# Hybrid decoder step on one core: expert section in one block with the router, stick-breaking attention and the front of the delta rule in one block, and a last expert pair of its own

## The reference, cut to what matters

```python
h = rms_norm(x, norm_mix); proj = h @ w_in          # columns: gated delta rule q k v z beta a, stick-breaking q k v
# delta rule, 8 heads x 64, in chunks of 64 tokens:
decay = exp(G_i - G_j)                              # G: cumulated log decays
low   = strict_lower(beta * k k^T * decay)          # t_inv = (I + low)^-1
qk    = lower(q k^T * decay)
u, w  = t_inv @ (v * beta), t_inv @ (k * beta * exp(G))
# then the state recurrence over 4 chunks, per-head norm, gate silu(z)
# stick-breaking attention: z = q k^T / 8 + b, A[t,s] = sigmoid(z[t,s]) * prod_{s<j<t} sigmoid(-z[t,j]), o = A v
#   (sampled tokens: over 1024 cached keys and values read by page; prompt: within its 256 tokens)
x = x + concat(o_delta, o_attention) @ w_out
# 32 experts, top 4 per token:
hu = t @ w_up[e] + b_up[e]; act = (up + 1) * gate * sigmoid(1.702 * gate); y = act @ w_down[e] + b_down[e]
x = x + sum_e gate_weight * y;  output rms_norm(x, norm_final)
```

## Time and profile before

| what | us |
|---|---|
| median of 3 runs | 1319.24 (1318.08 to 1328.87) |
| the profiled execution, its own time | 1323.29 |
| its span, first to last instruction | 1321.7 |
| TensorE busy | 1254.5 (95%) |
| VectorE, ScalarE, GpSimd busy | 406.7, 240.7, 92.2 |
| moved by DMA | 463.58 MB, mean 351 GB/s |

### The profile page before, as it was taken

The page is one execution under the profiler, slowest core; times in us unless marked ns, Lnnn a source line. Parts: engine busy times, 40 slices in busy tenths (PEclk is TensorE's granted clock), DMA queues, the critical chain, the costliest instruction groups (busy, mean ns, idle before and its releaser), DMA issues.

```text
span 1321.7 us, 19961 instructions
## 1 busy us (share of the span) xinstructions
PE 1254.5 (95%) x7888; PEld 571.3 (43%) x7888; DVE 406.7 (31%) x921; ACT 240.7 (18%) x402; POOL 92.2 (7%) x167
## 2 busy tenths in 40 slices
PE   8999999799999999999999999999999999999996
PEld 6777766587433333333333333333333333333332
DVE  4721424552742222322122232212213222222224
ACT  3222333323211011110111011011101101010103
POOL 6101141152000000000000000000000000000000
PEclk9999998889989999999999999999999999999999
DMA  9643699100779999999999999999999999999993
GB/s 324 229 133 112 219 387 360 30 20 7 286 264 381 429 427 428 428 428 429 428 428 428 428 428 428 429 428 429 428 428 429 428 428 428 428 428 429 428 428 139
DMA packets 66105, 463.58 MB, mean 351 GB/s; under 512 B 16654, under 2 KB 16782, under 8 KB 41478
## 3 DMA queue, kind: packets, MB, share of 16 engines
q1 hardware_dynamic: 62808, 452.22, 83.4%
q0 software_dynamic: 3200, 10.49, 2.1%
q10 hardware_dynamic: 46, 0.18, 0.0%
HBM read 459.15 MB, written 3.70 MB: 350 GB/s over the span
## 4 chain that ended last, share of the span: by engine, by line
PE 47%; DMA 23%; DVE 1%; issue 1%; SPq 0%; ACT 0%; POOLq 0%; POOL 0%; DVEq 0%; ACTq 0%
PE bank L2064 28%; DMA ring<-in_w_up 20%; PE bank L2081 6%; PE bank L2033 4%; PE bank L2012 4%; DMA hoT<-in_w_down 2%; PE bank L2016 1%; PE bank L2037 1%; PE bank L2108 1%; PE bank L2053 0%; PE bank L2089 0%; PE bank L2119 0%; SPq L750 0%; DVE work L2297 0%; DVE X L2292 0%
## 5 line engine op out<-in xcount | busy, mean ns | idle before, releaser
L2064 PE MATMUL bank<-ring,work 128*64 128x512 f32 x1536 | 340.1, 597 | 14.6 <-DMA ring<-in_w_up 14.6
L2064 PEld LDWEIGHTS bank<-ring,work 128*64 128x64 f32 x1536 | 109.3, 137 | 242.8 <-issue 230.5
L2081 PE MATMUL bank<-ring,work 128*64 128x512 f32 x768 | 173.0, 596 | 7.4 <-ACT work L2171 5.5
L410 PE MATMUL bank<-hoT,ring 128*128 128x288 f32 x448 | 113.0, 407 | 1.1 <-ACT hoT L445 0.8
L2064 PE MATMUL bank<-work 128*64 128x512 f32 x256 | 112.9, 594 | 0.0
L2064 PE MATMUL bank<-hoT,work 128*64 128x512 f32 x256 | 112.9, 594 | 0.0
L2263 DVE TENSOR_SCALAR work<-bank 128x512 f32<-128x512 f32 x32 | 21.9, 683 | 257.8 <-PE bank L2064 257.8
L2081 PEld LDWEIGHTS bank<-ring,work 128*64 128x64 f32 x768 | 55.7, 137 | 103.0 <-issue 99.1
L410 PEld LDWEIGHTS bank<-hoT,ring 128*128 128x128 f32 x448 | 83.5, 190 | 23.2 <-ACT hoT L445 0.9
L2155 ACT ACTIVATE work<-bank 128x1024 f32<-128x1024 f32 x16 | 16.4, 1023 | 383.2 <-PE bank L2016 383.2
L2225 DVE TENSOR_TENSOR X<-X,bank 128x512 f32<-128x512 f32 x64 | 44.0, 688 | 108.6 <-PE bank L2033 108.6
(11 more groups left out here) (396 smaller groups left out, 1315.5 us busy)
## 6 DMA issues: line engine op xcount, KB each, us to landing
ring<-in_w_up SPq DMA_DIRECT2D x96, 2048.0 KB, 24.6
ring<-in_w_down SPq DMA_DIRECT2D x48, 2048.0 KB, 26.9
work<-in_w_up SPq DMA_DIRECT2D x16, 2048.0 KB, 25.8
hoT<-in_w_up SPq DMA_DIRECT2D x16, 2048.0 KB, 30.1
work<-in_w_down SPq DMA_DIRECT2D x8, 2048.0 KB, 25.1
hoT<-in_w_down SPq DMA_DIRECT2D x8, 2048.0 KB, 29.4
ring<-in_w_in SPq DMA_DIRECT2D x7, 2048.0 KB, 16.7
ring<-in_cache_k SPq DMA_DIRECT2D x48, 256.0 KB, 3.1
```

What stands on the lines that cost most here:

```text
L410: ins = pe.matmul(bank[0:m, i % 2, 0:T], w[:, k, :], hT[:, k, :], start=k == 0, stop=k == KD - 1)
L2064: ins = pe.matmul(bank[CAP * e:CAP * e + CAP, g, :], xT[:, k, CAP * e:CAP * e + CAP], weight(odd, ch + e, k % 2 * RSLOT + 512 * g), start= ...
L2081: ins = pe.matmul(bank[CAP * e:CAP * e + CAP, 4 + m, :], aT[:, k, CAP * e:CAP * e + CAP], weight(odd, ch + e, k % 4 * D + 512 * m), start= ...
```

## The change

Four things.

- **No barrier before the expert section.** Its streams follow the router's in the same block. In the barrier's place stand waits: all five engines wait for `s_passes` (the number of passes is written), GpSimd clears its two buffers once the second tile's choice is made, SyncE loads the last norm's weight once the six norm rows are made, VectorE waits for the stored states only before it writes the first activation. The two spare products at the end of the router (`keep_busy(2, 2)`) are gone.
- **Attention and delta-rule front joined.** What stood at the head of block 4 now stands among the attention's work of block 3: `decay_columns`, `decay_rows(i)`, `products(c)` on TensorE, each through bank 7 of PSUM; `copy_rows`, `exp_differences` on ScalarE; `differences`, `take_products`, `lower` on VectorE; three additions and the first level's masks on GpSimd. Keys and values are both turned into bank 6 and both copied by ScalarE (`copy_kv`); `scale_v` is gone, and GpSimd scales the values later, in block 4. Eight spare products stand at three places of the joined block. Some of its tiles lie in the ring, in the buffer of chunk 3, so chunk 3 is now loaded at the head of block 4. There ScalarE makes the row exponentials from a copy in one activation of 1280 columns (`eR`), after the copies of `turn_T`. The biases of the experts are loaded after the heads' norm, before chunks 0, 1 and 6.
- **One more unit of the cache by GpSimd** (unit 11).
- **The last pair by itself.** TensorE's loop runs one turn less, and the last two pairs stand behind it. In the very last, the gather and turn for a pair that does not come are left out, and prompt tile 0 of X is put into banks 6 and 7, where its last outputs are accumulated; ScalarE squares and VectorE scales it from there. For all pairs, the last two slices of `up` are done by halves of the columns. The final norm's operations are in another order, with fused ones for the sampled tokens and tile 0.

```diff
-        BY_POOL = [m for m in range(12, 32) if m % 2]
+        BY_POOL = [m for m in range(11, 32) if m % 2]
...
-                sp.wait_ge(s_ringfree, U_WO)
-                load_chunk(sp, 0, 3)
...
+                def decay_columns():
+                    for i, (mp, md) in enumerate(((U2, dU2), (Us2, dUs2))):
+                        pe.matmul(bank[:, 7, NU * i:NU * i + 16], mp, gg[:, 0:16], start=True, stop=True)
+                        ins = pe.matmul(bank[:, 7, NU * i + 16:NU * (i + 1)], md, gg[:, 16:NU], start=True, stop=True)
+                    ins.then_inc(d_R, 1)
+
+                def decay_rows(i):
+                    g = GROUPS[i]
+                    if i:
+                        pe.wait_ge(d_D, i)
+                        pe.wait_ge(d_eGT, i)
+                    else:
+                        pe.wait_ge(d_Gs, 1)
+                    pe.wait_ge(d_pool, i + 1)
+                    pe.matmul(bank[:, 7, 0:width(g)], blk64, Lm[:, cols(g)], start=True, stop=True).then_inc(d_R, 1)
+
+                def products(c):
+                    if c:
+                        pe.wait_ge(d_QK, c)
+                    else:
+                        pe.wait_ge(d_D, 3)
+                        pe.wait_ge(d_eGT, 3)
+                    for p in range(HP):
+                        for a in range(2):
+                            ins = pe.matmul(bank[pr(a), 7, P * p:P * p + P], gq[pr(a), 4 + p, tk(c)], gq[pr(a), p:p + 5:4, tk(c)],
+                                            start=True, stop=True)
+                    ins.then_inc(d_KK, 1)
...
                 scores(0)
+                decay_columns()
                 scores(1)
+                decay_rows(0)
                 turn_kv(0)
                 turn(0)
                 turn_kv(1)
                 values(0)
+                decay_rows(1)
                 turn(1)
                 scores(2)
+                decay_rows(2)
+                values(1)
                 turn_kv(2)
-                values(1)
+                products(0)
                 turn(2)
                 scores(3)
+                products(1)
+                values(2)
                 turn_kv(3)
-                values(2)
+                products(2)
+                keep_busy(3)
                 turn(3)
                 turn_kv(4)
                 values(3)
+                products(3)
+                keep_busy(1)
+                products(4)
+                keep_busy(4)
...
                 betas(0)
                 betas(1)
-                copy_k(0)
+                copy_kv(0)
+                copy_rows(0)
                 copy_A(0)
-                copy_k(1)
+                copy_kv(1)
+                copy_rows(1)
                 copy_A(1)
                 betas(2)
-                copy_k(2)
+                copy_rows(2)
+                exp_differences(0)
+                exp_differences(1)
+                copy_kv(2)
                 copy_A(2)
                 betas(3)
-                copy_k(3)
+                copy_kv(3)
                 copy_A(3)
-                copy_k(4)
+                copy_kv(4)
+                exp_differences(2)
...
+                def differences(i):
+                    g = GROUPS[i]
+                    u0, u1 = GRP[g]
+                    dve.wait_ge(d_R, i + 2)
+                    dve.tensor_tensor(un(QK)[:, u0:u1], un(bank[:, 7, 0:width(g)]), ubc(Gs, u0, u1), ALU.subtract).then_inc(d_D, 1)
+                    dve.wait_ge(d_D, i + 1)
+                    dve.scalar_tensor_tensor(out=un(E1)[:, u0:u1], in0=un(QK)[:, u0:u1], scalar=-1.0,
+                                             in1=mbc((nS, nS, dnS)[i], u1 - u0), op0=ALU.mult, op1=ALU.add).then_inc(d_A1, 1)
+
+                def take_products(k):
+                    KQ = bank[:, 7, :].rearrange("p (u two j) -> p u two j", u=HP, two=2)
+                    u = slice(4 * k, 4 * k + 4)
+                    dve.wait_ge(d_KK, k + 1)
+                    c(dve.tensor_tensor(un(Lb)[:, u], KQ[:, :, 1], ubc(bet, 4 * k, 4 * k + 4), ALU.mult))
+                    dve.wait_ge(d_E2, k // 2 + 1)
+                    dve.tensor_tensor(un(QK)[:, u], KQ[:, :, 0], un(QK)[:, u], ALU.mult).then_inc(d_QK, 1)
+
+                def lower(i):
+                    g = GROUPS[i]
+                    u0, u1 = GRP[g]
+                    dve.wait_ge(d_E1, i + 1)
+                    dve.tensor_tensor(Lb[:, cols(g)], Lb[:, cols(g)], E1[:, cols(g)], ALU.mult).then_inc(d_L, 1)
+                    dve.wait_ge(d_L, i + 1)
+                    c(dve.scalar_tensor_tensor(out=un(Tb)[:, u0:u1], in0=un(Lb)[:, u0:u1], scalar=-1.0, in1=mbc(LVL[:, 0, :], u1 - u0),
+                                               op0=ALU.mult, op1=ALU.mult))
+                    dve.tensor_tensor(un(Tb)[:, u0:u1], un(Tb)[:, u0:u1], mbc(I64, u1 - u0), ALU.add).then_inc(d_T[g], 1)
...
+                dve.wait_ge(d_R, 1)
+                c(dve.tensor_copy(Gs, bank[:, 7, 0:2 * NU]))
+                dve.sem_inc(d_Gs, 1)
                 weights(0)
-                scale_v(0)
+                differences(0)
                 weights(1)
-                scale_v(1)
+                differences(1)
                 copy_heads(0)
-                scale_v(2)
+                differences(2)
                 weights(2)
                 copy_heads(1)
-                scale_v(3)
+                take_products(0)
+                take_products(1)
+                lower(0)
                 weights(3)
                 copy_heads(2)
-                scale_v(4)
+                take_products(2)
+                take_products(3)
                 copy_heads(3)
+                lower(1)
+                take_products(4)
+                lower(2)
...
+                load_chunk(sp, 0, 3)
                 sp.dma_start(rw, router_w[0].rearrange("(p k) e -> p k e", k=KD)).then_inc(s_rw, 16)
...
-                keep_busy(2, 2)
...
+                act.activation(eR, eR, ACT.Exp).then_inc(d_eGT, 1)
+                pool.tensor_tensor(un(vb), un(vb), ubc(bet, 0, NU), ALU.mult).then_inc(d_pool, 1)
...
-        with nc.Block() as block:
+                eng.wait_ge(s_passes, 3 + 1)
+                sp.wait_ge(s_nrow, 6)
+                pool.wait_ge(d_pool, SCALED["decode_rows_doubled"])
+                pool.wait_ge(s_mk, 2)
                 pool.memset(PGT, 0.0)
...
+                def up_by_half(i, mm, odd):
+
+                    for e in range(2):
+                        arrived(mm, odd, 6 + e)
+                    for half in range(2):
+                        for k in (KD - 2, KD - 1):
+                            for g in (2 * half, 2 * half + 1):
+                                for e in range(2):
+                                    ins = pe.matmul(bank[CAP * e:CAP * e + CAP, g, :], xT[:, k, CAP * e:CAP * e + CAP],
+                                                    weight(odd, 6 + e, k % 2 * RSLOT + 512 * g), start=False, stop=k == KD - 1)
+                                    if g == 3 and k == KD - 1:
+                                        ins.then_inc(s_wused, 1)
+                        if half == 0:
...
+                    if last:
+                        for m in range(2):
+                            ins = pe.matmul(bank[:, 6 + m, :], ident[:], X[:, 0, 512 * m:512 * (m + 1)], start=True, stop=True)
+                        ins.then_inc(M["gathered"], 1)
+                    else:
+                        gather(i + 2)
...
-                with pe.Fori(0, n * (NPAIR // 2)) as mm:
+                with pe.Fori(0, n * (NPAIR // 2) - 1) as mm:
                     body(mm, 0)
                     body(mm, 1)
+                more = pe.value_load(npass[0:1, 1:2], min_val=0, max_val=-(-T // CAP) - 1)
+                body(more * (NPAIR // 2) + (NPAIR // 2 - 1), 0)
+                body(more * (NPAIR // 2) + (NPAIR // 2 - 1), 1, True)
...
+                for t in range(2):
+                    for m in range(2):
+                        pe.matmul(bank[:, LAST_BANK[t] + m, :], PGT[:, t * P:(t + 1) * P], oo[:, 512 * m:512 * (m + 1)],
+                                  start=t == 1, stop=True, skip_group_check=True).then_inc(M["y"], 1)
...
+                dve.wait_ge(s_wb, 48)
+                dve.wait_ge(M["y"], base + 1)
+                for m in range(2):
+                    x = X[0:ND, 2, 512 * m:512 * (m + 1)]
+                    dve.tensor_tensor(x, x, bank[ND * m:ND * m + ND, 0, :], ALU.add).then_inc(M["y_added"], 1)
+                shift_mean(0)
+                rstd_of(0)
+                dve.wait_ge(M["y_added"], base + 2)
+                dve.scalar_tensor_tensor(out=yrow(2), in0=X[0:ND, 2, :], scalar=fstat[0:ND, 2, 4:5], in1=wb[0:ND, :],
+                                         op0=ALU.mult, op1=ALU.mult).then_inc(s_yrow, 1)
+                shift_mean(1)
+                for m in range(2):
+                    x = X[:, 1, 512 * m:512 * (m + 1)]
+                    dve.wait_ge(M["y"], base + 4 + m)
```

(9 more changed lines are left out.)

287 lines of the change are left out of this document (122 added, 165 removed).

## The result

| | median us (runs) | ratio to before, 95% interval |
|---|---|---|
| before, in the same group | 1322.13 (10 runs, 1314.20 to 1328.87) | |
| changed kernel | 1311.74 (10 runs, 1310.44 to 1314.37) | 0.9925 [0.9906, 0.9943] |
| before, in the group of a second chip | 1323.20 (17 runs, 1317.31 to 1329.12) | |
| changed kernel once more, in that group | 1310.68 (6 runs, 1307.73 to 1312.79) | 0.9915 [0.9887, 0.9942] |

The change gains 0.75 to 0.85% by the ratios, and 10.4 and 12.5 us by the medians of the two groups, a group being the runs that were taken together on one chip. I had forecast 14.6 us. I had also given 0.54 to a time under 1306.0 and 0.42 to one above it that does not lose; it came out above. The profiled execution took 1310.44 us, 12.9 less than that of before; this pair can be compared stretch by stretch.

A forecast was written before the change was run, and what follows sets the result against it. Engine order was taken to bound a front of some 380 us, then an 885 us weight stream hanging on the first up product. Gains 2.7 + 6.6 + 3.4 + 0.9 + 1.0 = 14.6 off 1319.24 gave 1304.5 us, range 1297 to 1313.

The forecast's parts named there:

- part 1, unit 11: Sampled cache pages: GpSimd issues unit 11 early, DMA fills 150 to 157 us; 2.7 us gained, bounds 0 and 4.8.
- part 2, joined block to level product: Block 3's first product to first level product: 49.2 us in place of 55.8, 6.6 gained, bounds 1 to 10.1.
- part 2, chunk 3 in the thin slices: Head of block 4: SyncE's chunk 3 moves into slices of 30 GB/s and less, at no cost.
- part 3, barrier: Expert section's entry: first up product at 378.0 against 381.37, 3.4 us gained, bounds 2.0 and 4.5.
- part 3, clock behind it: First 32 up products: without TensorE's idle gap, half the clock loss saved, 0.9 us, bounds 0 and 1.8.
- part 4, tail: Behind the last down: reordered final norm issues the store at 1317.6 against 1318.58, 1.0 us gained, bounds 0.3 and 1.8.
- The walk: Joined block: VectorE's order of work with its waits takes 40.0 us at 2.4 GHz, 42.5 with 2.5 added for the clock.
- The first: Joined block takes 47 us, through bank 7's handoffs and half clock; its gain is 1 to 2, time 1310; chance 0.16.
- The second: Weight stream keeps its time, as DMA sets the loop's first 30 us; only the tail counts, 1318 us; chance 0.05.
- the fourth: Joined block runs in lockstep across three engines, 59 us, and the kernel is slower at 1321 to 1326; chance 0.04.
- The third: ScalarE's table switches in the joined block drain, 4.1 us longer, `weights(3)` 2.8 late, 1307.3 us; chance 0.07.

The follow-up runs named there:

- The kernel with the clock at 1.00 throughout: Changed kernel with weight chunk 3 loaded behind block 4's prompt-state stores, plus four spare products at the last value pages and own heads: 1304.32 us, ratio 0.9854.

## Why the prediction was right, and where it was not

1311.7 lies in the range, 1304.5 was 7.2 us too low. Of these, 2.9 are the starting point: I took the gain from a median of three runs, 1319.24, and ten runs have 1322.13. The other 4.2 are gain that did not come: 14.6 forecast, 10.4 measured. The terms, by my own steps:

| step | forecast | measured in the pair of profiles |
|---|---|---|
| part 1, unit 11 | 2.7 | 1.3 |
| part 2, joined block to level product | 6.6 | 7.1 |
| part 2, chunk 3 in the thin slices | 0, "free" | -2.5 |
| part 3, barrier | 3.4 | 3.9 |
| part 3, clock behind it | 0.9 | 1.7 |
| part 4, tail | 1.0 | 1.5 |
| sum | 14.6 | 13.0, of the pair's 12.9 |

The sum is nearer than its terms. Two were too large, by 1.4 and 2.5 us, and four too small, by 0.5, 0.5, 0.8 and 0.5, which hides more than half of the miss; that the errors cancelled so far is luck.

- **Part 1.** The size failed. "Filled from 150 to 157, DMA gains 1.1 MB": the windows of the changed kernel, to be read against the earlier trace rows, are

```profile
150.00:157.00 7.00, 7.00 (x126) 6.06 (x117) 3.63 (x4) 2.05 (x2) 1.54 (x3) 1.00 1.01 326
157.00:160.00 3.00, 3.00 (x51) 2.63 (x50) 1.23 (x1) 1.45 (x2) 0.61 (x2) 1.00 1.01 335
160.00:180.00 20.00, 20.00 (x301) 15.57 (x303) 9.88 (x11) 8.63 (x11) 8.07 (x15) 1.00 1.01 359
```

  The gap was filled to 326 GB/s and not to 385, 0.7 MB, and from 157 to 180 the rate is now 335 and 359 where it was 385, so 0.7 MB were given back. What stays is what moved ahead of 150 us (259 GB/s from 145 to 150, against 208 before), 0.3 MB or 0.7 us. That the end of the stage hangs on DMA (the 0.38 us at 213.05) was right: the last page is 0.5 us earlier, and the stall has moved from the keys to the values. The other 0.8 of the 1.3 us lie between that page and r, and the whole term is no larger than the scatter of r.
- **Part 2.** The walk gave 42.5 us for the block and 6.3 from there to the level product. The profile has 43.7 to the end of the last `lower` and 4.7 behind it. The kernel with the clock at 1.00 throughout took 40.8 to block 4's first product, the walk's 40.0 plus the barrier. So the walk was right at full clock, and the 2.5 us that I had added for the clock are lost at the block's start (clock 0.57 in 218 to 226). The spare products hold the second half; by the medians they are worth 1.7 to 3.4 us, which is not clear of noise.
- **Chunk 3.** This step of the prediction failed; it reads "into the slices of 30 GB/s and less, free". I had asked whether DMA had room for the chunk and not who else used DMA there. TensorE runs some 350 matmul instructions in 10 us at this place, and a packet of instructions comes each 3.3 to 4 us; 50 us later, in 310 to 320, it runs 40, and the same chunk costs nothing that the waits show. The term was 0 and measured 2.5 us in this pair.
- **Part 3.** Right in place and nearly in size. With the gap gone, the whole clock term was saved, 1.7 us, close to the upper bound of 1.8 and not the half that I took.
- **Part 4.** The walk in the earlier trace rows was too careful by half a us: VectorE was through with the last product with `wb` 17.1 us behind the last landing, where the walk had 17.6.
- **Rivals.** The first (a block of 47 us) is out: 44. The second fell with chunk 12's 11.4 us, the fourth with 48.7 us. The third needed 1.4 us beside each table load. The timeline of ScalarE in the joined block shows the load and the next activation with nothing between:

```profile
238.45 1.28 ACT L1214 ACT_TABLE_LOAD   x1
239.75 0.63 ACT L1214 ACTIVATE work<-work 128x512 f32<-128x512 f32 x1
```

  The activation ahead of it ended at 238.44. The 1.38 us of drain that the Trainium skill states (ScalarE: Activation LUTs, "What ACT_TABLE_LOAD costs") does not appear; its 1.28 of load does.
- The other 2.5 us between 12.9 and the medians' 10.4 are the choice of the pair: the profiled execution of the changed kernel was its fastest of ten, that of the kernel before 1.2 us over its median.
